# Constant multiplications at TensorE's barriers, and a modulation pair moved ahead of the last turning, in a two-layer hybrid backbone

## The reference

```
for l in range(DEPTH):                                        # DEPTH = 2
    mod_l = s_lat @ w_mod[l] + b_mod[l];  mod_c = s_ctx @ w_mod[l] + b_mod[l]
    hl = _layer_norm(xl) * (1.0 + sc1) + sh1                  # the same for the context, hc
    yl, yc = _token_mixing(hl, hc, need_ctx, ...)
    xl = _layer_norm(alpha * xl + g1 * yl, ln1_g[l], ln1_b[l])
    if need_ctx: xc = _layer_norm(alpha * xc + cg1 * yc, ...)  # layer 0 alone
    hl = _layer_norm(xl) * (1.0 + sc2) + sh2
    ml = _expert_choice_ffn(hl, w_router[l], w_exp_gate[l], w_exp_up[l], w_exp_down[l])
    xl = _layer_norm(alpha * xl + g2 * ml, ln2_g[l], ln2_b[l])
```

## Time and profile before

| | us |
|---|---|
| median of 3 runs | 3837.84 |
| lowest and highest run | 3831.02, 3839.59 |
| the profiled execution | 3853.39 |
| its span | 3851.7 |
| TensorE matrix records busy, share of the span | 3421.1, 89% |
| VectorE busy | 2324.1, 60% |
| ScalarE busy | 1624.9, 42% |
| GpSimd busy | 1046.6, 27% |
| mean granted TensorE clock | 0.945 |

### The profile page before, as it was taken

How to read it: one execution, slowest core, us unless ns; L and a number is a source line. 1 busy time by engine, 2 the same in 40 slices (tenths; PEclk the granted TensorE clock), 3 DMA queues, 4 the chain that set the end, 5 groups by cost and what they waited for, 6 DMA issues and landing times.

```text
span 3851.7 us, 49012 instructions
## 1 busy us (share of the span) xinstructions
PE 3421.1 (89%) x19072; PEld 2795.1 (73%) x19072; DVE 2324.1 (60%) x3395; ACT 1624.9 (42%) x2095; POOL 1046.6 (27%) x640
## 2 busy tenths in 40 slices
PE   7998898999999869899987299998999959999994
PEld 4997678988887757677766288678766757777773
DVE  2786742511112649999998684833232348998997
ACT  3114743411111246666664322744211126667763
POOL 2001012221211125555553200122222104444442
PEclk8989999999999889999999599998999979999997
DMA  7242133012212439889888122121222219999994
GB/s 242 99 146 80 45 99 121 23 61 88 83 60 83 138 126 308 301 309 311 309 303 291 62 88 77 50 88 44 72 74 90 99 56 314 332 329 341 334 330 177
DMA packets 331926, 633.91 MB, mean 165 GB/s; under 512 B 14526, under 2 KB 104910, under 8 KB 325358
## 3 DMA queue, kind: packets, MB, share of 16 engines
q1 hardware_dynamic: 309056, 557.88, 42.2%
q0 software_dynamic: 22704, 73.73, 5.8%
HBM read 615.05 MB, written 16.50 MB: 164 GB/s over the span
## 4 chain that ended last, share of the span: by engine, by line
PE 64%; DVE 15%; issue 8%; ACT 5%; POOL 3%; DMA 3%; POOLq 1%; DVEq 0%; ACTq 0%; SPq 0%
PE ps L850 41%; PE ps L1256 11%; DVE part L2084 3%; POOL part L796 2%; PE ps L980 2%; PE ps L1012 2%; DVE area L1687 1%; PE ps L998 1%; ACT hx L1527 1%; DVE hx L2084 1%; DMA raw<-in_w_exp_down 1%; ACT area L1379 1%; DVE area L2111 1%; DVE area L2092 1%; PE ps L1000 1%
## 5 line engine op out<-in xcount | busy, mean ns | idle before, releaser
L850 PE MATMUL ps<-hx,part 128*128 128x384 f32 (+2 forms) x4704 | 930.6, 356 | 11.2 <-POOL part L518 5.5
L850 PEld LDWEIGHTS ps<-hx,part 128*128 128x128 f32 x4704 | 831.1, 189 | 99.1 <-issue 23.2
L1256 PE MATMUL ps<-part,hx 128*128 128x512 f32 x3072 | 781.0, 407 | 105.0 <-POOL part L796 72.7
L1256 PEld LDWEIGHTS ps<-part,hx 128*128 128x128 f32 x3072 | 586.4, 195 | 256.5 <-POOL part L796 87.3
L2084 DVE TENSOR_TENSOR part<-raw,part 128x2048 fp32r<-128x2048 f32 (+1 forms) x256 | 587.1, 2296 | 118.1 <-ACT part L1527 115.8
L1527 ACT ACTIVATE part<-raw 128x2048 fp32r<-128x2048 f32 x256 | 490.2, 1916 | 142.7 <-PE ps L1256 119.5
L518 POOL TENSOR_TENSOR part<-raw,part 128x2048 fp32r<-128x2048 f32 x52 | 238.0, 4577 | 821.7 <-ACT part L515 821.6
L1256 PE MATMUL ps<-hx 128*128 128x512 f32 x1536 | 375.0, 393 | 6.6 <-DVE hx L2084 6.4
L1256 PEld LDWEIGHTS ps<-hx 128*128 128x128 f32 x1536 | 289.3, 189 | 75.7 <-DVE hx L2084 8.0
L2084 DVE TENSOR_TENSOR hx<-raw,hx 128x2048 fp32r<-128x2048 f32 (+1 forms) x128 | 308.1, 2407 | 58.9 <-ACT hx L1527 58.3
L850 PE MATMUL ps<-part,hx 128*128 128x256 f32 (+2 forms) x2208 | 317.2, 306 | 18.9 <-DVEq L532 15.5
(11 more groups left out here) (260 smaller groups left out, 3930.2 us busy)
## 6 DMA issues: line engine op xcount, KB each, us to landing
raw<-in_w_exp_gate SPq DMA_DIRECT2D x128, 1024.0 KB, 5.2
raw<-in_w_exp_up SPq DMA_DIRECT2D x128, 1024.0 KB, 5.6
raw<-in_w_exp_down SPq DMA_DIRECT2D x128, 1024.0 KB, 5.2
raw<-in_w_mod SPq DMA_DIRECT2D x48, 1024.0 KB, 6.9
raw<-in_w_in SPq DMA_DIRECT2D x44, 1024.0 KB, 5.4
raw<-in_w_gate SPq DMA_DIRECT2D x32, 1024.0 KB, 8.0
area<-in_bias POOLq DMA_DIRECT2D x32, 512.0 KB, 4.1
raw<-in_w_branch SPq DMA_DIRECT2D x16, 1024.0 KB, 7.3
```

What stands on the lines that cost most here:

```text
L850: last = mm(dst, a, b, start=i == 0, stop=i == len(pairs) - 1)
L1256: last = mm(ps[:, bank, :], x, y, start=kh == 0 and a == 0, stop=kh == 1 and a == len(pairs) - 1)
```

## The change

`leave` takes a function that is called between the engine's own signal and its wait. TensorE passes `busy(bank, count=4)` at barriers AB, attention, D, mLSTM, gate, merge, out, router and gather of both layers, which makes 18 of its 22 barriers. `busy` multiplies the 128x128 identity with 512 columns of constants, all float32, `count` times, into a bank of PSUM that nobody reads: 4 times, at barrier out 2 times. A further call of 8 multiplications stands ahead of the wait for `slots`. Ahead of barrier merge TensorE also waits for the last but one group's `z_part`, which frees the bank. And of the leftover pairs, `mod_pair(7, 1)` moves from t = 7 to t = 6, ahead of the last turning and behind `mod_pair(7, 0)`.

```diff
-            def leave(self):
+            def leave(self, meanwhile=None):
 
                 self.eng.drain().then_inc(stage, 1)
                 self.k += 1
+                if meanwhile:
+                    meanwhile()
                 self.eng.wait_ge(stage, 4 * self.k)
...
+                def busy(bank, count=4):
+
+                    def run():
+                        for _ in range(count):
+                            mm(ps[:, bank, :], ident, consts[:, 0:4 * P], start=True, stop=True)
+                    return run
+
...
-                st.leave()
+                st.leave(busy(1))
 
                 us, gs = head_pairs(l), turn_groups(l)
...
-                st.leave()
+                pe.wait_ge(*S("z_part", l).at(g - 1))
+                st.leave(busy(2))
...
-                    if l == 0 and t >= full:
-                        mod_pair(7, t - full)
+                    if l == 0 and t == full:
+                        mod_pair(7, 0)
+                        mod_pair(7, 1)
...
-                st.leave()
+                st.leave(busy(5, 2))
...
                     mod_pair(7, 2)
                     mod_pair(7, 3)
+                busy(5, 8)()
                 pe.wait_ge(*S("slots", l).at(1))
...
-                st.leave()
+                st.leave(busy(5))
```

More of the change, by code:

```diff
@@ L1016, in _ @@
                             values(g)
-                st.leave()
+                st.leave(busy(0))
                 cuts = even if full == NT else [(0, LAT, 0)]
```

## The result

The changed kernel takes 3852.41 us in the median of 9 runs, against 3842.25 us for the kernel before on the same chips (9 runs). The ratio is 1.0028, 95% interval 1.0017 to 1.0039, which is +10 us, and 6.5 to 15.0 by the interval. That is inside the range of the prediction. The 7.7 us (0.2%) that I had set for no change lie within the interval, and the median is above them.

The account below looks back on a forecast made before the run. TensorE, with 64% of the chain, was taken to bound the kernel, idle gaps and granted clock included. Delays of 23.0 us less gains of 17.0 gave +6.0 on the 3837.84 median: 3843.8 us, range 3833 to 3856.

Parts of the forecast that it names:

- two kinds of barriers: TensorE waits 0.44 to 1.87 us at AB, attention, mLSTM, gate; 3.1 to 8.5 at others, 15.95 for the slots.
- Price of one multiplication: Each float32 product costs 0.86 us at full clock; four delay the eight short barriers by 21.6 us in all.
- Rival 3: Multiplications are cheaper than the D stage's form or overlap the signals' arrival: -4.6 us, 3833; chance 0.09.
- near -3 us: Whole sum if four multiplications took 0.86 us by the skill's figure, the eight short barriers costing 2.8 us together.
- Longer barriers: No delay at D, merge, gather and slots; 0.3 + 0.4 us at barrier out, 0.7 at router in layer 1.
- The moved pair: In layer 0, without the pair between the last logits, everything behind barrier out comes 3.5 us earlier.
- Rival 4: Second pair's blocks land later than 1319.7 and push the turning: 0.5 to 3 us, sum +7 to +9; no separate chance.
- Clock gains: Half-clock stretches avoided: output projection 4.4 us, gather 4.8, gate of layer 0 1.7, merge of layer 0 1.1, attention 1.5.
- Attention: In the attention loop one group of scores a layer is spared half clock, gaining 1.5 us in all.
- mLSTM: Clock gain in mLSTM, which begins with small products and long waits: nothing taken, 0 to 1.5 us a layer possible.
- Rival 1: The clock doesn't hold in the idle time left; output, merge, attention and half the gather gains go: +15.4 us, 3853; chance 0.25.
- The sum: Whole kernel: delays 23.0 us less gains 17.0, net +6.0, put on the median as 3843.8.

Follow-up runs that it names:

- short_waits: Changed kernel with constant multiplications only at AB, attention, mLSTM, gate and out, and the pair moved back; 3862.36 us against 3842.49, ratio 1.0052.
- long_waits: Changed kernel with constant multiplications only at D, merge, router, gather and ahead of the slots, the pair not moved; 3833.62 us, ratio 0.9979.
- after: The changed kernel itself, with the whole change against the kernel before; 3852.41 us, ratio 1.0028.
- e4_after: The changed kernel with 4 of 16 experts, otherwise whole; 2887.24 us, +10.4 against e4_before.
- e4_long_and_pair: Changed kernel with 4 of 16 experts, long waits filled, pair moved, no multiplications at AB, attention, mLSTM, gate, out; 2865.41 us, -11.4 against e4_before.
- before: The kernel before, without the change; median 3842.25 us beside the changed kernel's runs, profiled execution 3853.39 us.
- e4_before: The kernel before with 4 of the 16 experts in each layer, the base for the other 4-expert kernels; 2876.80 us.
- long_pair_no_gather: Changed kernel without multiplications at AB, attention, mLSTM, gate, out and gather, the pair still moved; 3838.38 us, ratio 0.9983 against the kernel before.
- pair_only: The kernel before with the moved pair alone, no multiplication of constants; 3839.59 us against 3842.49, ratio 0.9996.

## Why the prediction was right, and where not

- **What bounds the kernel, two kinds of barriers.** Right. The multiplications cost at the short waits (short_waits +20) and gain at the long ones (long_waits -8.9): the two halves of the change, each run alone, lie clear of no change on opposite sides.
- **Price of one multiplication.** Right: 3.44 for four by the row, 3.43 or 3.44 in four places and 3.53 and 3.56 behind barrier AB. The 216 ns that the Trainium skill's page TensorE: Matmul & The Clock Gate, section Back-to-back issue gap, gives for an isolated product of 512 columns at full clock is a quarter of the 0.86 us measured for this float32 product; the measurement decides. Rival 3 falls with it. The sum of "near -3 us" beside that figure was worked out wrongly: 21.6 less 2.8 is 18.8, and +6.0 less 18.8 is -12.8, with the other terms kept.
- **Longer barriers.** Right: the gaps cover them. The margins were as worked out at barrier router, 1.11 us left in layer 0. At barrier out in layer 0 the two cost nothing, since another arrival had taken TensorE's place there.
- **The moved pair.** Mechanism right, size 3.5 forecast, 2.4 to 3.2 seen. The sentence that failed is that the other engines had nothing left in the stage that was as late: GpSimd's store landed late, beside the loads that the moved pair lets start earlier. I had seen that SyncE fetches the fourth pair sooner, and wrote that nobody waits for it; nobody does, but the store travels at the same time. Rival 4 feared the second pair's blocks: the pair did wait for them, until 1320.90 in after, but the turning at 1324.82 then waited 1.99 us for VectorE, so nothing was pushed.
- **Clock gains.** Output 4.4 forecast; the stages show 2.6 in layer 1, and 5.44 in layer 0 with the pair in it. Gather 4.1 net forecast, 4.0 seen. Gate 1.7 forecast; the stage is +0.21 in layer 0 and +1.66 in layer 1, so 1.5 seen. Merge 1.1 forecast, 1.6 seen. These two sizes are right, the reason given for them only in part: short_waits gets them with its own barriers filled, and long_waits gets them in layer 0 with these barriers empty. Attention 1.5 forecast, nothing seen: the loop's first tiles are thin themselves, and the clock fell all the same. mLSTM nothing forecast, 2.3 seen. The last two errors nearly cancel, and that was luck.
- **Rival 1** fell in the profile of the changed kernel, and came back twice: in e4_after and e4_long_and_pair the clock was lost at the output projection of layer 1 when the weights came 1.3 us later. Its ground, that the clock had fallen once in two after 1.87 us, told less than I took it for: long_waits has the same two gaps with the two clocks exchanged.
- **The sum**, +6.0, agrees with the stages, +5.6, in part because the errors of attention and mLSTM cancel. The medians say +10, with 6.5 as the interval's lower end, and the 4.6 between them is about the size of the noise of the runs. The last sentence of the prediction, that nothing here touches the expert loops, was too strong. Nothing in their code is touched, but the clock at their start is another one: the second block of layer 0 took 5.49 instead of 3.02. Whether the loops cost the changed kernel anything isn't shown; in its own trace they are 3.55 longer in layer 0 and 6.61 shorter in layer 1. I called it no change, if barely, and gave slower 0.43; by the median it is slower by more than 7.7 us.

## What to carry to other kernels

Filling a wait pays where the wait is longer than the filling. At a short wait it can keep the clock too, but costs more than the clock gives back. Give each barrier its own count from its measured gap. Here four multiplications cost some 3.1 us at each barrier with half a microsecond of wait, and the eight short barriers ate more than all the gains. And when an engine takes a transfer's data sooner, ask what goes out on the queues in its place and whose store or load is on the way then.

## What the runs showed of the hardware

Most stages outside the experts repeat within 0.1 us from trace to trace where the same clock is granted (stage D of layer 0 120.38 in before, 120.38 in e4_before, 120.40 in long_pair_no_gather). The attention of layer 0 is an exception, 195.15 in before and 194.10 in pair_only. Medians of 5 to 12 runs leave some 4 us open. For edits of a few us a table of stage lengths from the traces tells more than the runs do.

A slower clock can go with a shorter stage: the last expert of layer 0 took 53.2 us with its second block at 0.50 and 56.0 at 1.00, and the five traces with a slow second block are the five shortest of the 14.

After an idle time of 1.80 us ahead of the output projection the clock stayed at 1.00 in after, and after 2.92 us it stood at 0.50 from 1.4 us behind the resumption in e4_after. But equal idle times don't give equal clocks: behind 1.87 us at the gate projection it stood at 1.00 in one layer and fell in the other, and before and long_waits differ in which.
